# A two-layer trunk on one core: paired visits on TensorE, and the last column in two halves

## The chip, the core and the metric

The kernel runs on one core of a Trainium2 chip. The core has a matrix engine (TensorE, PE), a vector engine (VectorE, DVE), a scalar engine (ScalarE, ACT), GpSimd (POOL) and SyncE (SP). Each has a queue of its own that it works through in order, and each can issue DMAs. TensorE reads its operands from SBUF and writes to PSUM, which has 8 banks of 512 float32 values per partition. The metric is the device time of one execution in microseconds; lower is better.

## What is computed

Two layers and a final norm over 256 tokens of width 2048, in float32:

```python
for i in range(DEPTH):                       # DEPTH = 2
    h = _rms_norm(x, norm_mix[i])
    if i % 2 == 0:
        x = x + _gmlp_mixer(h, ...)          # u * (W_s v + b) in chunks of 128 tokens, then w_out
    else:
        x = x + _s5_mixer(h, ...)            # 128 groups of 16 channels, 64 complex states each
    x = x + _swiglu(_rms_norm(x, norm_ffn[i]), ffn_w1[i], ffn_w3[i], ffn_w2[i])
    gate = jax.nn.sigmoid(_rms_norm(x, norm_ple[i]) @ ple_w_gate[i])
    x = x + gate * (p[i] @ ple_w_proj[i])
return _rms_norm(x, norm_final)
```

In the S5 mixer the states follow a diagonal recurrence, s[t] = a s[t-1] + B u[t], and the output is Re(C s) + d u, then gelu and a gated product.

## The kernel before

**Weight tiles.** All large weights stream through SBUF in 792 tiles of 256 x 512 (`STAGES`, `ORDER`). SyncE loads a tile into RAW, ScalarE writes its rounded copy WHI (line 810), VectorE the rest WLO (line 1096). ScalarE and VectorE are some four tiles ahead of TensorE. TensorE multiplies a tile in 12 matmuls of 512 columns, eight with WHI (line 1616) and four with WLO (line 1622). The operands, in OP, are split in the same way; the helper `high` writes the one part on ScalarE and `low` the other on VectorE. `start(stage, n)` is the number of the first tile of column n of a stage; `split_used` counts the tiles that TensorE has finished.

**Visits.** Small matmuls stand between two tiles, where a table of tile numbers puts them. In the first layer these are the turns of x (`turn`, 0 to 3), two turns of the mixing weights WN (`turn_ws`, at `WT_AT`) and four mixes (`mix`, at `MIX_AT`, all into banks 6 and 7, one per column of stage "us").

**The state stage.** It begins at tile 396, W0, the start of "win" (32 tiles, x into u), and runs into "out1". A step g is the tile W0 + g. Each of the engines has a loop over g in which its jobs stand in a fixed order. The channels go in eight duos d of 256. For a duo:
- TensorE computes the increments of the states from u (`into_states`, lines 1793 on, at `INTO_AT`), and later, from the scanned states, the output (`out_of_states`, lines 1809 on, at `OUT_AT`). Increments of duo d need the tables TQ and the spread input UP; the output needs the tables TD and TK, the states SD, and that ScalarE has taken the output of duo d - 1 from PSUM.
- VectorE takes the increments from PSUM (CV, line 1501) and scans them (lines 1510 to 1525, ten instructions) at `INTO_AT + 1`; at `OUT_AT + 2` it turns the output (YG, line 1532, `turn_y`), and one step later it writes the low part of the operand (line 1537, `y_low`).
- ScalarE takes the output with gelu at `OUT_AT + 1` (YP, line 1011, `take_y`) and writes the high part of the operand at `OUT_AT + 2` (line 1018, `y_high`), for which it waits for YG.
- u comes in four parts of two duos. ScalarE stores part n to DRAM (`ud`, line 995, `store_u`) at step 8n + 11, and at step 8n + 13 it waits for that store and issues four loads that spread it into UP (line 1003, `spread_u`).
- GpSimd loads the tables TQ, TD, TK and TE at the steps of `TQ_AT`, `TD_AT`, `TK_AT` and `TE_AT`, and waits in order for the buffer of each: table TD of duo 5, at step 30, waits for the output of duo 3.

Where a loop has two duos at a step, the lower one's job comes first:

```python
INTO_AT = [W0 + g for g in (16, 19, 24, 27, 32, 34, 40, 42)]
OUT_AT = [W0 + g for g in (20, 23, 28, 31, 36, 38, 44, 46)]
```

**The end.** The last column of "gate1" has all its nine tiles in SBUF. TensorE goes through them once for the first 128 tokens and once for the others, 54 matmuls of 512 columns each (lines 1882 to 1884). Behind each half come a sigmoid (line 1072), product, sum and statistics on VectorE (lines 1589 to 1591), the norm, and the DMA of the output.

## Time and profile before

| | |
|---|---|
| runs | 2236.19, 2233.8, 2236.26 us; median 2236.19 |
| the profiled execution | 2234.53 us, of which the span of the trace is 2232.5 |
| TensorE busy | 2217.6 us, 99% of the span; granted clock 0.999 |
| VectorE busy | 1443.7 us, 65% |
| ScalarE busy | 1024.3 us, 46% |
| GpSimd busy | 493.6 us, 22% |
| DMA | 531.02 MB, mean 238 GB/s |

The span runs from the first to the last instruction of the trace, and the rest of an execution's time lies around it. All rows below come from that one execution, with times in us from the span's start. A row of a timeline is a run of equal instructions: its start, how long it lasts, the engine, the line, the operation, what is written from what, and how often; in brackets how long the engine stood idle before, and what released it. ACTq is a DMA issue from ScalarE's queue. Busy TensorE says little about waits of a fraction of a microsecond, since matmuls overlap in the pipe; the distance between starts tells more.

### The profile page before, as it was taken

The numbers are of one execution on the slowest core, as the hardware profiler recorded it, in microseconds if no ns is written. First come the engines' busy times: TensorE is split into PE (matmuls) and PEld (weight loads), VectorE is DVE, ScalarE is ACT, GpSimd is POOL, SyncE is SP. The second block draws the span as 40 slices with busy tenths as digits, with TensorE's granted clock in tenths as the row PEclk, the third lists the DMA queues.
The fourth block names the chain that finished last, engine by engine and source line by source line (L and its number), as shares of the span: only waits on it lengthen the run. The fifth ranks groups of instructions, "written<-read, shape, count | busy, mean of one in ns | idle before, by whom it ended". The sixth has DMA issues, their size and how long they took to land.

```text
span 2232.5 us, 28320 instructions
## 1 busy us (share of the span) xinstructions
PE 2217.6 (99%) x11226; PEld 1830.5 (82%) x11226; DVE 1443.7 (65%) x1608; ACT 1024.3 (46%) x1233; POOL 493.6 (22%) x470
## 2 busy tenths in 40 slices
PE   9999999999999999999999999999999999999998
PEld 7888888888888888888887788888888888888886
DVE  7878776666666666666668866555555445556665
ACT  5544444444434444445444445544444344444454
POOL 1246145456665534301003100000000000000001
PEclk9999999999999999999999999999999999999999
DMA  8677898988888898888689877777776667777773
GB/s 304 186 207 228 264 283 249 257 249 237 259 248 225 243 280 247 265 244 269 231 261 353 307 227 217 216 223 220 211 218 206 194 194 225 220 210 233 230 233 143
DMA packets 350676, 531.02 MB, mean 238 GB/s; under 512 B 106209, under 2 KB 127089, under 8 KB 349905
## 3 DMA queue, kind: packets, MB, share of 16 engines
q1 hardware_dynamic: 339456, 491.64, 73.7%
q0 software_dynamic: 8320, 30.75, 3.7%
q10 hardware_dynamic: 2768, 6.83, 0.9%
q8 instruction: 88, 1.44, 0.3%
q14 instruction: 44, 0.35, 0.1%
HBM read 475.67 MB, written 53.48 MB: 237 GB/s over the span
## 4 chain that ended last, share of the span: by engine, by line
PE 97%; DMA 1%; DVE 1%; issue 0%; ACT 0%; SPq 0%; ACTq 0%; DVEq 0%
PE PS L1616 63%; PE PS L1622 31%; DMA RAW<-in_s_w_out 1%; DMA HT<-zd 0%; PE PS L1883 0%; PE PS L1884 0%; PE PS L1882 0%; PE PS L1721 0%; PE PS L1647 0%; PE PS L1710 0%; DVE OP L1122 0%; PE PS L1830 0%; PE PS L1805 0%; PE PS L1822 0%; PE PS L1756 0%
## 5 line engine op out<-in xcount | busy, mean ns | idle before, releaser
L1616 PE MATMUL PS<-WHI,OP 128*128 128x512 f32 x6208 | 1538.4, 390 | 0.2
L1096 DVE TENSOR_TENSOR WLO<-RAW,WHI 128x1024 fp32r<-128x1024 f32 x783 | 1016.5, 1312 | 692.7 <-ACT WHI L810 688.1
L1616 PEld LDWEIGHTS PS<-WHI,OP 128*128 128x128 f32 x6208 | 1161.9, 188 | 244.7 <-issue 3.4
L810 ACT ACTIVATE WHI<-RAW 128x1024 fp32r<-128x1024 f32 x783 | 827.9, 1062 | 997.4 <-PE PS L1622 644.4
L1622 PE MATMUL PS<-WLO,OP 128*128 128x512 f32 x3104 | 829.8, 389 | 0.9 <-DVE WLO L1096 0.9
L1622 PEld LDWEIGHTS PS<-WLO,OP 128*128 128x128 f32 x3104 | 582.5, 188 | 122.3 <-DVE WLO L1096 1.4
L794 POOL TENSOR_TENSOR ON<-X,GF 128x1024 f32<-128x1024 f32 x3 | 9.9, 3295 | 941.8 <-DVE X L1448 941.8
L696 POOL TENSOR_TENSOR TA<-BRAW,FAC 128x64 f32<-128x64 f32 x16 | 10.7, 669 | 268.4 <-DMA BRAW<-in_s_b_im 268.3
L858 ACT ACTIVATE S<-PS,RC 128x512 f32<-128x512 f32 x66 | 41.7, 684 | 37.3 <-PE PS L1622 37.1
L1122 DVE SCALAR_TENSOR_TENSOR OP<-HT,VEC,OP 128x128 fp32r<-128x128 f32 x120 | 37.9, 388 | 14.1 <-ACT OP L834 14.0
L1108 DVE TENSOR_TENSOR OP<-HT,OP 128x512 fp32r<-128x512 f32 x50 | 36.2, 764 | 14.5 <-ACT OP L825 14.5
L825 ACT ACTIVATE OP<-HT 128x512 fp32r<-128x512 f32 x50 | 28.8, 624 | 28.3 <-DMA HT<-zd 28.0
L834 ACT ACTIVATE OP<-HT,VEC 128x256 fp32r<-128x256 f32 x60 | 25.6, 498 | 18.9 <-DMA HT<-zd 18.9
L1163 DVE BATCH_NORM_STATS2 STAT<-X 128x6 f32<-128x512 f32 x54 | 34.0, 670 | 0.0
L1435 DVE SCALAR_TENSOR_TENSOR Z<-PS,RC,S 128x512 f32<-128x512 f32 x44 | 30.8, 741 | 4.0 <-PE PS L1622 4.0
L1147 DVE STREAM_TRANSPOSE ZT<-Z 128x512 f32<-128x512 f32 x50 | 32.6, 691 | 0.9
L733 POOL TENSOR_TENSOR TB<-CT,LAMA 128x512 f32<-128x512 f32 x16 | 29.0, 1811 | 0.0
L712 POOL TENSOR_TENSOR QT<-TA,TB 128x512 f32<-128x512 f32 x16 | 27.5, 1717 | 1.3
L1387 DVE TENSOR_TENSOR X<-X,PS 128x1024 f32<-128x1024 f32 x20 | 24.4, 1219 | 4.4 <-PE PS L1622 4.4
L946 ACT ACTIVATE EXPF<-PS 128x128 f32<-128x128 f32 (+7 forms) x128 | 16.8, 319 | 21.1 <-PE PS L1721 21.1
L734 POOL TENSOR_TENSOR DT<-TA,TB 128x512 f32<-128x512 f32 x16 | 25.9, 1618 | 1.3
L732 POOL TENSOR_TENSOR TA<-CT,LAMA 128x512 f32<-128x512 f32 x16 | 25.8, 1612 | 1.3
(214 smaller groups left out, 942.1 us busy)
## 6 DMA issues: line engine op xcount, KB each, us to landing
RAW<-in_ffn_w SPq DMA_DIRECT2D x528, 512.0 KB, 4.4
RAW<-in_gm_w_in SPq DMA_DIRECT2D x64, 512.0 KB, 4.3
RAW<-in_s_w_out SPq DMA_DIRECT2D x64, 512.0 KB, 4.8
RAW<-in_ple_w_gate SPq DMA_DIRECT2D x56, 512.0 KB, 4.7
zd<-ZT SPq DMA_DIRECT2D x40, 512.0 KB, 3.6
HT<-zd SPq DMA_DIRECT2D x160, 128.0 KB, 5.0
RAW<-in_gm_w_out SPq DMA_DIRECT2D x32, 512.0 KB, 5.5
RAW<-in_s_w_in SPq DMA_DIRECT2D x32, 512.0 KB, 4.8
```

The source lines that it names most:

```text
L733: step(G_.tensor_tensor(TB[:, :, :, :], c(0), up(1), ALU.mult))
L810: A_.activation(hi_of(t), raw_of(t), ACT.Copy).then_inc(hi_ready, 1)
L825: A_.activation(OP[:, block_:block_ + QB, P * h:P * h + P].rearrange("p m (i a) -> p m i a", a=32), HT[:, :, :, h, :].rearrange("p i m a - ...
L858: last = A_.activation(dst(th), acc(stage, n)[:, th, :], func, scale=RC[:, RMS[stage], th:th + 1])
L1096: V_.tensor_tensor(lo_of(t), raw_of(t), hi_of(t).bitcast(F32), ALU.subtract).then_inc(lo_ready, 1)
L1108: V_.tensor_tensor(here[:, :, TOK + P * h:TOK + P * h + P].rearrange("p m (i a) -> p m i a", a=32), HT[:, :, :, h, :].rearrange("p i m a - ...
L1122: last = V_.scalar_tensor_tensor(OP[:, b, TOK + P * th:TOK + P * th + P].rearrange("p (i a) -> p i a", a=32), HT[:, :, m, th, :], VEC[:, r ...
L1147: last = V_.transpose(ZT[:, :, :, h, :], src[:, h, :].rearrange("p (m c a) -> p c m a", c=4, a=32))
L1163: last = V_.bn_stats(STAT[:, th, 6 * n:6 * n + 6], src[:, th, NW * n:NW * n + NW])
L1435: last = V_.scalar_tensor_tensor(Z[:, th, :], acc(stage, n)[:, th, :], RC[:, i_rms, th:th + 1], S[:, th, :], ALU.mult, ALU.mult)
L1616: T_.matmul(dst[:, th, :], x_part, hi_of(t)[:, f], start=first and kk == 0 and part == 0, stop=False)
L1622: last = T_.matmul(dst[:, th, :], hi, lo_of(t)[:, f], start=False, stop=last_one and kk == TK - 1)
```

## The change

- **Head.** ScalarE and VectorE write the first half of the first operand, then split weight tile 0, then write the second half. On TensorE the turns 2 and 3 of x both stand behind tile 1 (before: behind tiles 0 and 2).
- **First layer.** Both turns of WN stand behind one tile, into banks 6, 7 and 4, 5. The mixes 0 and 1 share a tile, and 2 and 3, in banks 6 and 4 in turn.
- **State stage.** `INTO_AT` and `OUT_AT` of the first four duos are four tiles apart, so that the increments of duo d + 1 and the output of duo d stand behind one tile for d = 0 to 3, increments first. VectorE's take of the last increments comes one step earlier, right behind the scan of duo 6, and `y_low` of duo 5 one step later. The tables' steps move with them in part.
- **End.** The second 128 tokens of the last column go in two parts of 256 columns each, which have banks of their own; the statistics have a fifth group, and a part of ON is filled ahead.
- GpSimd also waits for six tiles of "up0a" before it clears EXP[1].

```diff
-MIX_AT = [start("us", n) + 6 for n in range(NT)]
+MIX_AT = [start("us", n - n % 2) + 6 for n in range(NT)]
+MIX_BANK = [6, 4, 6, 4]
...
-WT_AT = [start("v", 2) + 2, start("v", 2) + 6]
+WT_AT = start("v", 2) + 2
...
+PARTS = [(0, 0, NW), (1, 0, NW // 2), (1, NW // 2, NW)]
...
-INTO_AT = [W0 + g for g in (16, 19, 24, 27, 32, 34, 40, 42)]
-OUT_AT = [W0 + g for g in (20, 23, 28, 31, 36, 38, 44, 46)]
-
-TAKEN_AT = [t + 1 for t in INTO_AT[:DUOS - 1]] + [INTO_AT[DUOS - 1]]
+INTO_AT = [W0 + g for g in (16, 20, 24, 28, 32, 34, 40, 42)]
+OUT_AT = [W0 + g for g in (20, 24, 28, 32, 36, 38, 44, 46)]
+
+TAKEN_AT = [t + 1 for t in INTO_AT[:DUOS - 1]] + [INTO_AT[DUOS - 1] - 1]
+LOW_AT = [t + 3 + (d == DUOS - 3) for d, t in enumerate(OUT_AT)]
...
-TQ_AT += [(W0 + g, W0 + g + 1) for g in (17, 20, 25, 28, 33, 35)]
+TQ_AT += [(W0 + g, W0 + g + 1) for g in (17, 21, 25, 29, 33, 35)]
...
+                    pool.wait_ge(split_used, start("up0a") + 6)
                     step(G_.memset(EXP[1][:, :, :, :], 0.0))
...
-            high(0)
+            high(0, (0,))
             section()
+            high(0, (1,))
             section()
...
-                    if W0 + g == Y_AT[d] + 1:
+                    if W0 + g == LOW_AT[d]:
                         y_low(d)
...
             def prologue(t):
-                if t in (0, 2):
-                    turn({0: 2, 2: 3}[t])
+                if t == 1:
+                    turn(2)
+                    turn(3)
...
                 for d in range(DUOS):
                     if t == INTO_AT[d]:
                         into_states(d)
+                for d in range(DUOS):
                     if t == OUT_AT[d]:
                         out_of_states(d)
...
-            for th in range(2):
+            for th, c0, c1 in PARTS:
...
-                        f = slice(NW * kk, NW * kk + NW)
+                        f = slice(NW * kk + c0, NW * kk + c1)
```

**TensorE's queue around steps 19 to 24.** First the kernel before. L1805 are increments, L1822 and L1830 an output; SD_126 is the states' buffer of the even duos, SD_127 of the odd ones.

```order
L1805 MATMUL PS<-TQ_114,UP_131 32x64 x32
L1616 MATMUL PS<-WHI,OP 128x512 x8
L1622 MATMUL PS<-WLO,OP 128x512 x4
L1822 MATMUL PS<-TK_118,UP_131 32x128 x16
L1830 MATMUL PS<-TD_115,SD_126 32x128 x32
...
L1822 MATMUL PS<-TK_119,UP_131 32x128 x16
L1830 MATMUL PS<-TD_116,SD_127 32x128 x32
L1616 MATMUL PS<-WHI,OP 128x512 x8
L1622 MATMUL PS<-WLO,OP 128x512 x4
L1805 MATMUL PS<-TQ_113,UP_132 32x64 x32
```

The same place after, where L1825 are increments and L1842 and L1850 an output:

```order
L1636 MATMUL PS<-WHI,OP 128x512 x8
L1642 MATMUL PS<-WLO,OP 128x512 x4
L1825 MATMUL PS<-TQ_114,UP_131 32x64 x32
L1842 MATMUL PS<-TK_118,UP_131 32x128 x16
L1850 MATMUL PS<-TD_115,SD_126 32x128 x32
...
L1642 MATMUL PS<-WLO,OP 128x512 x4
L1825 MATMUL PS<-TQ_113,UP_132 32x64 x32
L1842 MATMUL PS<-TK_119,UP_131 32x128 x16
L1850 MATMUL PS<-TD_116,SD_127 32x128 x32
L1636 MATMUL PS<-WHI,OP 128x512 x8
```

The increments of duo 1 have moved down by a tile, onto the tile behind which the output of duo 0 stands, and the output of duo 1 has moved down by a tile behind the increments of duo 2.

**ScalarE's queue from step 24 on, before.** Z is u being taken from PSUM, YP the output of duo 1, OP<-YG its operand, ud the third store of u, and UP_131<-ud the spread of it:

```order
L858 ACTIVATE Z<-PS,RC 128x512 x2
L1011 ACTIVATE YP<-PS 128x2x16x8 x2
L810 ACTIVATE WHI<-RAW 128x1024
L1018 ACTIVATE OP<-YG 128x2x256
L810 ACTIVATE WHI<-RAW 128x1024 x2
L995 DMA ud<-UT 128x1024
L810 ACTIVATE WHI<-RAW 128x1024 x2
L1003 DMA UP_131<-ud 32x2x512 x4
L1011 ACTIVATE YP<-PS 128x2x16x8 x2
```

The same after:

```order
L869 ACTIVATE Z<-PS,RC 128x512 x2
L821 ACTIVATE WHI<-RAW 128x1024
L1023 ACTIVATE YP<-PS 128x2x16x8 x2
L821 ACTIVATE WHI<-RAW 128x1024
L1030 ACTIVATE OP<-YG 128x2x256
L821 ACTIVATE WHI<-RAW 128x1024
L1007 DMA ud<-UT 128x1024
L821 ACTIVATE WHI<-RAW 128x1024 x2
L1015 DMA UP_131<-ud 32x2x512 x4
L1023 ACTIVATE YP<-PS 128x2x16x8 x2
```

The take of YP, the operand and the tile split between them have moved down by one tile split; the store and the spread of u stand where they stood, now with one split instead of two between the operand and the store.

**VectorE's queue at steps 25 to 27, before.** UT is u turned for the store, YG the turned output of duo 1, CV the increments of duo 2, SD_126 the end of their scan (ten rows from CV to there), OP<-YG the low part of the operand:

```order
L1096 TENSOR_TENSOR WLO<-RAW,WHI 128x1024 x2
L1497 STREAM_TRANSPOSE UT<-Z 128x1024
L1532 STREAM_TRANSPOSE YG<-YP 128x512
L1501 STREAM_TRANSPOSE CV<-PS 128x8x2x32
...
L1525 TENSOR_TENSOR SD_126<-CV,CA 128x8x31
L1096 TENSOR_TENSOR WLO<-RAW,WHI 128x1024
L1537 TENSOR_TENSOR OP<-YG,OP 128x2x256
```

The same after:

```order
L1110 TENSOR_TENSOR WLO<-RAW,WHI 128x1024 x2
L1512 STREAM_TRANSPOSE UT<-Z 128x1024
L1516 STREAM_TRANSPOSE CV<-PS 128x8x2x32
...
L1540 TENSOR_TENSOR SD_126<-CV,CA 128x8x31
L1110 TENSOR_TENSOR WLO<-RAW,WHI 128x1024
L1547 STREAM_TRANSPOSE YG<-YP 128x512
L1110 TENSOR_TENSOR WLO<-RAW,WHI 128x1024
L1552 TENSOR_TENSOR OP<-YG,OP 128x2x256
```

The turn into YG, on which ScalarE's operand waits, stood ahead of the scan of duo 2 and now stands behind it and one more tile split. At steps 33 to 35 the same has happened to the turn of duo 3 and the scan of duo 4.

## Rows read from the trace of the kernel before

**Rows 1.** the page: its span, and the busy time of TensorE
```profile
span 2232.5 us, 28320 instructions
PE 2217.6 (99%) x11226; PEld 1830.5 (82%) x11226; DVE 1443.7 (65%) x1608; ACT 1024.3 (46%) x1233; POOL 493.6 (22%) x470
```

**Rows 2.** timeline, TensorE, state stage: start us, us, engine, line, operation, tiles, count
```profile
1180.02 1.98 PE L1616 MATMUL PS<-WHI,OP 128*128 128x512 f32 x8
1182.74 1.98 PE L1616 MATMUL PS<-WHI,OP 128*128 128x512 f32 x8
...
1185.55 1.08 PE L1822 MATMUL PS<-TK,UP 128*32 128x128 f32 x32
...
1187.65 2.11 PE L1616 MATMUL PS<-WHI,OP 128*128 128x512 f32 x8
```

**Rows 3.** timeline, ScalarE and its DMA issues (ACTq), third store of u
```profile
1192.81 1.18 ACT L1018 ACTIVATE OP<-YG 128x512 fp32r<-128x512 f32 x1 [3.04 <-DVE YG L1532]
...
1194.82 0.33 ACTq L995 DMA_DIRECT2D ud<-UT  x1
...
1203.74 2.62 ACTq L1003 DMA_DIRECT2D UP<-ud  x4
```

**Rows 4.** timeline of VectorE beside it
```profile
1192.10 0.67 DVE L1532 STREAM_TRANSPOSE YG<-YP 128x512 f32<-128x512 f32 x1
1192.70 0.68 DVE L1501 STREAM_TRANSPOSE CV<-PS 128x512 f32<-128x512 f32 x1
...
1194.02 0.69 DVE L1511 TENSOR_TENSOR CB<-CV,TE 128x512 f32<-128x512 f32 x1
1194.74 0.42 DVE L1512 TENSOR_TENSOR CV<-CA,CB 128x256 f32<-128x256 f32 x1
...
1198.94 1.22 DVE L1096 TENSOR_TENSOR WLO<-RAW,WHI 128x1024 fp32r<-128x1024 f32 x1
```

**Rows 5.** line L995 at 1194.5 to 1195.5: that store, issue to landing
```profile
DMA to landing us min/median/max: 8.0/8.0/8.0
```

**Rows 6.** line L1003, 1205.5 to 1206.0: the spread that it feeds
```profile
DMA to landing us min/median/max: 7.6/8.3/8.9
```

**Rows 7.** windows: stretch, busy by engine (count), TensorE clock, DMA share, GB/s
```profile
1200.00:1205.00 5.00, 5.00 (x111) 3.94 (x110) 4.97 (x7) 1.06 (x1) 2.99 (x4) 1.00 1.03 413
```

**Rows 8.** timeline of TensorE: visits of steps 32 and 38, wait of 44
```profile
1219.51 1.10 PE L1805 MATMUL PS<-TQ,UP 128*32 128x64 f32 x64
...
1240.80 1.08 PE L1822 MATMUL PS<-TK,UP 128*32 128x128 f32 x32
...
1262.93 1.08 PE L1822 MATMUL PS<-TK,UP 128*32 128x128 f32 x32 [0.69 <-DVE CV L1501]
```

**Rows 9.** timeline of ScalarE: the fourth store of u and its spread
```profile
1223.88 0.33 ACTq L995 DMA_DIRECT2D ud<-UT  x1
...
1235.02 2.54 ACTq L1003 DMA_DIRECT2D UP<-ud  x4
```

**Rows 10.** timeline of TensorE: the first mix and the tile behind it
```profile
120.44 1.95 PE L1710 MATMUL PS<-V,WT 128*128 128x128 f32 x16
122.14 2.08 PE L1616 MATMUL PS<-WHI,OP 128*128 128x512 f32 x8
```

**Rows 11.** timeline of all engines: the end of the program
```profile
2223.04 0.69 ACT L1072 ACTIVATE S<-PS,RC 128x512 f32<-128x512 f32 x1 [5.46 <-PE PS L1884]
...
2223.76 0.69 DVE L1589 TENSOR_TENSOR Z<-S,PS 128x512 f32<-128x512 f32 x1 [8.31 <-ACT S L1072]
...
2227.01 1.15 ACT L1079 ACTIVATE ON<-ON,RC 128x1024 f32<-128x1024 f32 x1 [0.23 <-DVE RC L1596]
```

**Rows 12.** windows of TensorE: the 54 matmuls of the last row half
```profile
2210.62:2223.00 12.38, 12.38 (x55) 1.00 0.20 85
```

**Rows 13.** timeline of all engines: the start
```profile
9.15 2.08 PE L1616 MATMUL PS<-WHI,OP 128*128 128x512 f32 x8
...
15.59 0.76 POOL L643 DMA_DIRECT2D PN<-in_p  x1 [5.16 <-DMA X<-in_x]
```

More of the change, by code:

```diff
@@ L270, in trunk @@
         RHO = place("RHO", [P, PAIRS])
-        STAT = place("STAT", [P, 2, 4 * 6])
+        STAT = place("STAT", [P, 2, 5 * 6])
         MV = place("MV", [P, 2, 2])
@@ L469, in acc, with gate_of, proj_of @@
             return PS[:, b:b + 2, :]
+        def gate_of(th, c0, c1):
+            bank = BANKS["gate1", NT - 1] + th if c0 == 0 else 4
+            return PS[:, bank, c0:c1]
+        def proj_of(th, c0, c1):
+            return PS[:, 6 + th if c0 == 0 else 5, c0:c1]
         def feature_major(bank, h):
@@ L819, in high @@
                     act.wait_ge(ht_in, 64 * (MOVED.index(q) + 1))
-                for h in range(2):
+                for h in halves:
                     if bank is not None:
@@ L1067, in _ @@
             until(TILES)
-            for th in range(2):
-                act.wait_ge(half_done, th + 1)
-                A_.activation(S[:, th, :], acc("gate1", NT - 1)[:, th, :], ACT.Sigmoid, scale=RC[:, 5, th:th + 1]).then_inc(half_s, 1)
+            for i, (th, c0, c1) in enumerate(PARTS):
+                act.wait_ge(half_done, i + 1)
+                A_.activation(S[:, th, c0:c1], gate_of(th, c0, c1), ACT.Sigmoid, scale=RC[:, 5, th:th + 1]).then_inc(half_s, 1)
+                if c1 < NW:
+                    continue
                 act.wait_ge(ms_ready, 7 + th)
@@ L1100, in until, with low @@
                     section()
-            def low(q):
+            def low(q, halves=(0, 1)):
                 stage, n, _, block_, row, _, bank = QUADS[q]
-                for h in range(2):
+                for h in halves:
                     dve.wait_ge(operand_hi, 2 * q + h + 1)
@@ L1166, in moments @@
             def moments():
-                V_.bn_aggr(MV[:, 0, :], STAT[:, 0, :])
-                step(V_.bn_aggr(MV[:, 1, :], STAT[:, 1, :]))
+                V_.bn_aggr(MV[:, 0, :], STAT[:, 0, 0:6 * NT])
+                step(V_.bn_aggr(MV[:, 1, :], STAT[:, 1, 0:6 * NT]))
                 step(V_.tensor_tensor(MSQ[:, :], MV[:, :, 0], MV[:, :, 0], ALU.mult))
@@ L1585, in _ @@
             until(TILES)
-            f = slice(3 * NW, D)
-            for th in range(2):
-                dve.wait_ge(half_s, th + 1)
-                step(V_.tensor_tensor(Z[:, th, :], S[:, th, :], PS[:, 6 + th, :], ALU.mult))
-                step(V_.tensor_tensor(X[:, th, f], X[:, th, f], Z[:, th, :], ALU.add))
-                step(V_.bn_stats(STAT[:, th, 6 * NT - 6:6 * NT], X[:, th, f]))
-                step(V_.bn_aggr(MV[:, th, :], STAT[:, th, :]))
+            for i, (th, c0, c1) in enumerate(PARTS):
+                f = slice(3 * NW + c0, 3 * NW + c1)
+                chunk = 6 * (NT - 1 + (c0 > 0))
+                dve.wait_ge(half_s, i + 1)
+                step(V_.tensor_tensor(Z[:, th, c0:c1], S[:, th, c0:c1], proj_of(th, c0, c1), ALU.mult))
+                step(V_.tensor_tensor(X[:, th, f], X[:, th, f], Z[:, th, c0:c1], ALU.add))
+                if c1 < NW:
+                    V_.tensor_tensor(ON[:, th, f], X[:, th, f], GF[:, f], ALU.mult)
+                step(V_.bn_stats(STAT[:, th, chunk:chunk + 6], X[:, th, f]))
+                if c1 < NW:
+                    continue
+                step(V_.bn_aggr(MV[:, th, :], STAT[:, th, 0:chunk + 6]))
                 V_.scalar_tensor_tensor(MS[:, th:th + 1], MV[:, th, 0:1], MV[:, th, 0:1], MV[:, th, 1:2],
@@ L1709, in mix @@
                         h = QB * n + m
-                        last = T_.matmul(PS[:, 6 + th, P * m:P * m + P], WT[:, h, :], V[:, th, P * h:P * h + P], start=True, stop=True)
+                        last = T_.matmul(PS[:, MIX_BANK[n] + th, P * m:P * m + P], WT[:, h, :], V[:, th, P * h:P * h + P], start=True, stop=True)
                 last.then_inc(mixed, 1)
@@ L1771, in first_layer @@
                     turn_p(0)
-                for i in range(2):
-                    if t == WT_AT[i]:
-                        turn_ws(i)
+                if t == WT_AT:
+                    turn_ws(0)
+                    turn_ws(1)
                 for n in range(NT):
@@ L1867, in _ @@
             free("gate1", NT - 1)
-            for th in range(2):
+            for th, c0, c1 in PARTS:
                 for j in range(DEEP):
```

30 lines of the change are left out of this document (15 added, 15 removed).

## The prediction

> **What bounds the kernel now.** The page comes first: TensorE is busy 2217.6 of 2232.5 us [rows 1], so the program is TensorE's queue of matmuls, and a change can only shorten the two ends, the gaps around the small matmuls, or the waits. The timeline of TensorE comes second. A weight tile (12 matmuls of 512 columns) repeats every 2.72 us, as 1180.02 to 1182.74 shows [rows 2]. Only the places between tiles can move. Third come the timelines of ScalarE and VectorE around the state stage, because each works through its own queue in order there and feeds the visits. I count steps in that stage as the code does: step g is the weight tile W0 + g.
>
> **Merged visits of the state stage.** Step 23's tile should have ended at 1182.74 + 2.72 = 1185.46; the output visit starts at 1185.55, and the tile behind it takes 2.11 us instead of 1.98 for its first part [rows 2]. So a visit costs 0.09 + 0.13 = 0.22 us beyond its own matmuls. Four increments now share a tile with the output of the duo before: 4 x 0.22 = 0.9 us less (up to 1.5, if the drain of the small matmuls shrinks too). The last duo's increments are now taken before two other VectorE jobs, so the wait of 0.69 us at step 44 [rows 8] goes, 0.7 us. What is late next there is the scan of the same duo, which has two steps more.
>
> **Merged visits of the first layer.** The first mix issues 16 matmuls in 1.95 us and the next tile starts 1.70 us after the first of them [rows 10]. With 16 at about 0.11 us that is their own work, so merging two of four mixes, the two turns of WS and two turns of X gives at most 0.1 us. I take 0.1.
>
> **The head.** Tile 0 starts at 9.15 [rows 13]. Its weight split no longer stands behind the second half of the first operand, which I take as 0.3 us (bounds 0 and 0.4). From 8.85 two tiles run to 14.3 and the turn of the third quarter of X, now ahead of tile 2, to about 15.2. The last quarter of X is there just before 15.59, where GpSimd, which waited for it, goes on [rows 13]. That wait gives the 0.3 us back. Sum 0, bounds -0.3 and +0.3. The new wait of GpSimd for tile 101 costs nothing: it is over before C has come back from DRAM.
>
> **The tail.** Behind the last matmul stand a sigmoid, three VectorE operations of 512 columns, and small ones [rows 11]. At 256 columns a VectorE operation takes 0.42 instead of 0.69 us [rows 4]: 3 x 0.27 = 0.8 us. The sigmoid (0.69) loses about 0.2. The scaling of ON on ScalarE (1.15 us) stays and hides VectorE's wider one. Against it stands TensorE: 54 matmuls of 512 columns take 12.38 us, 0.229 each [rows 12]; now 108 of 256. If the cost is all columns they are free. If the part beyond half of 0.229, as 0.013 us of fixed cost, is paid twice, they cost 54 x 0.013 = 0.7 us. No row has such a matmul with this operand type; the far bound is 0.188 us each, a weight load's length, +7.9 us. The small f32 matmuls with a full weight load run at 0.11 us apart [rows 10], so I take +0.4. Tail: -0.6 (bounds -1.0 and +0.1 without the far one).
>
> The Trainium skill, "TensorE: Matmul & The Clock Gate", section "Back-to-back issue gap", gives a gap of columns / 2.4 + 2.5 ns: 109 ns for 256, which by an estimate from that page would make the 108 matmuls 0.6 us shorter than they are now. The trace's 0.229 us for 512 is over the page's 0.216, so the measured row is what I use.
>
> **What moves behind what.** This is the term that decides. Before, VectorE turned the output of duo 1 (YG, 1192.10) before it took the increments of duo 2 (CV, 1192.70) and worked through them until 1198.94 [rows 4]. ScalarE writes the operand as soon as YG is there (1192.81), splits a tile and stores u for the third time at 1194.82 [rows 3]. After, OUT 1 stands at step 24 and its turn at step 26, behind the scan of step 25. ScalarE stands in its queue at the operand of duo 1 meanwhile, and the store of u, two entries further on, stands behind it.
>
> Worked through, in times of the trace before: the scan still starts at about 1192.6. It gets a split more in front of it, but the increments are there earlier. So YG starts at 1192.6 + 6.2 + 1.15 = 1200.0, the operand follows 0.7 later, and the store at 1201.8 (one tile split fewer than the 2.72 us of [rows 3, 4]). The store takes 8.0 us to land [rows 5], at 1209.8. The spread takes 2.6 us to issue [rows 3], and its last part 8.3 more to land [rows 6]: about 1220. The increments of duo 4 at step 32 need it. TensorE comes there at 1179.8 + 3 x 2.72 = 1188.0, then two merged visits of 3.4 us and eight tiles of 2.72, at 1216.6. It waits there for some 3.5 us. Before, the same data were there at 1214.6, for a visit at 1219.51 [rows 8].
>
> The same happens once more for the fourth u. ScalarE is free of the third spread at 1212.4. The output of duo 2 and a split (2.1), a split and YG on VectorE (1.2), its operand and three ScalarE jobs beside five of VectorE put the scan of duo 4 at 1224.1. It ends at 1230.4, YG of duo 3 starts at 1231.5, and the store is at 1233.3 (it was 1223.88 [rows 9]). With 8.0 us to land and 2.6 for the spread, ScalarE takes the output of duo 4 from PSUM at 1243.9 to 1245.1, and OUT 5 at step 38 needs that bank. OUT 5 was at 1240.80 [rows 8]; it is now 4.3 us later, whatever the stall at step 32 was, because this chain doesn't run through TensorE. Tile 40 needs the output of duo 5, for 0.6 us more. With the 0.7 us of step 44 the stage ends 4.3 + 0.6 - 0.7 = 4.2 us later; the merged visits are within this, since they only let TensorE come earlier to the wait.
>
> **The sum** against the profiled execution (2234.53 us, span 2232.5): +4.2 - 0.1 + 0 - 0.6 = +3.5, so 2238.0 us. The median of the runs shown is 1.7 above that execution, at 2236.19; the same +3.5 gives 2239.7. About 0.2%, 4.5 us, is what a measurement of this kernel can tell from no change, so the forecast is a small loss inside it.
>
> **Rivals.**
> 1. The store and spread land in time. The chain has two landings of 8 us, taken while the DMA engines are full (share 1.03 [rows 7]). If GpSimd, which now waits for OUT 3 before its table loads, leaves the engines free and each landing took 4 us, both stalls vanish and what is left is -0.9 - 0.7 - 0.1 - 0.6 = -2.3: 2233.9. For it: the engines' load does fall in that gap. Against it: the tile loads alone keep them busy, and two stores in a row would have to be fast. Beside it, the Trainium skill, "DMA: Bandwidth & Descriptors", section "Anatomy of one DMA — SWDGE (gpsimd) path", fits 2.0 us plus bytes / 436e3 (for GpSimd's path). For 512 KB that is an estimate of 3.2 us a landing and this rival's time. The trace shows 8.0.
> 2. Slower by more than can be missed: GpSimd's table loads behind OUT 3 (one step later, and later still by the stall) and the fourth spread meet in one burst. The spread then lands 2 to 4 us after ScalarE issued it later than I take, and the increments of duo 6 at step 40 wait as well. They are due only about 1 us after the spread's landing. From 1 us more on each landing it decides. 4.2 + 3 - 0.7 = +6.5: 2242.7.
> 3. The short matmuls go by the weight load (0.188 us): +7.9 in place of +0.4 in the tail, 2247. The 0.11 us spacing of full weight loads [rows 10] speaks against it.
> 4. The merging does nothing for a visit (the 0.22 us stay) and the tail gains nothing: within 1 us of the forecast, since the chain above sets the stage anyway. It is part of the forecast's case.
>
> **How the numbers follow.** Forecast 0.63, rival 1 0.18, rival 2 0.15, rival 3 0.04. The forecast's case alone runs from 2237.5 to 2242, by 1 us each way on the two landings and the tail's bounds. A fifth of it lies over 2240.7. Slower: 0.15 + 0.04 + 0.13 = 0.32. Faster needs a time below 2231.7, under rival 1's own value: 0.03. Same: 0.65. The range takes in rival 1's value and nearly all of rival 2's: 2233.0 to 2242.7.
>
> **What would show it.** In the timeline after: the third store of u about 7 us later relative to the tile of step 27 than before; TensorE idle before the increments of step 32 by 2 to 5 us and before the output of step 38 by 1 to 4; no wait at step 44; ScalarE's longest waits for YG; and behind the last matmul 1 us less than the 9 us now. It would be wrong if the store of u went out before the scan of duo 2 ended, if its landing took under 5 us, or if the 108 matmuls took over 13 us.

## The result: 2238.8 us against 2236.0

The changed kernel takes 2238.81 us (median of 22 runs, 2237.33 to 2242.11), the kernel before 2236.03 us (22 runs). The ratio is 1.0014, with a 95% interval of 1.0008 to 1.002: a small loss, 2.8 us between the medians and 0.14% by the ratio (its interval is 1.8 to 4.5 us), under the prediction's bound of 0.2%. All profile readings below are of one execution each. The one of after takes 2239.38 us, its span is 2237.3 us against 2232.5.

The page of after, its span, the busy engines, and the queue of instruction fetches (queue, kind, packets, MB, share), which answer to [rows 1]:

```profile
span 2237.3 us, 28436 instructions
PE 2218.9 (99%) x11280; PEld 1835.7 (82%) x11280; DVE 1450.4 (65%) x1612; ACT 1023.4 (46%) x1234; POOL 492.9 (22%) x470
...
q8 instruction: 89, 1.46, 0.3%
```

TensorE's timeline of after at step 20 (start us, us, engine, line, operation, tiles, count; in brackets the idle time before and its releaser). Increments, output and the next tile, where before had one visit with 0.22 us around it [rows 2]:

```profile
1175.22 1.10 PE L1825 MATMUL PS<-TQ,UP 128*32 128x64 f32 x64
...
1177.13 1.06 PE L1850 MATMUL PS<-TD,SD 64*32 64x128 f32 x52
1179.16 0.44 PE L1850 MATMUL PS<-TD,SD 64*32 64x128 f32 x12 [0.96 <-issue]
1179.53 2.11 PE L1636 MATMUL PS<-WHI,OP 128*128 128x512 f32 x8
```

The output stops for 0.96 us after 52 of its last 64 matmuls, and no other engine is named. The same timeline at steps 32, 38 and 40 (before: [rows 8]):

```profile
1219.08 1.10 PE L1825 MATMUL PS<-TQ,UP 128*32 128x64 f32 x64 [0.20 <-issue]
...
1220.99 1.16 PE L1850 MATMUL PS<-TD,SD 64*32 64x128 f32 x64
1224.53 2.09 PE L1636 MATMUL PS<-WHI,OP 128*128 128x512 f32 x8 [2.38 <-ACT WHI L821]
...
1246.15 1.08 PE L1842 MATMUL PS<-TK,UP 128*32 128x128 f32 x32 [1.45 <-ACT YP L1023]
...
1251.92 2.11 PE L1636 MATMUL PS<-WHI,OP 128*128 128x512 f32 x8 [0.65 <-ACT YP L1023]
```

Behind the visit of step 32 TensorE stands still for 2.4 us, at the output of step 38 for 1.45, ahead of tile 40 for 0.65. The releaser "WHI" of the first is not to be believed: ScalarE had finished that tile's split at 1214.69, 9.8 us earlier.

ScalarE's timeline of after, with its DMA issues, at the third and the fourth store of u (before: [rows 3], [rows 9]):

```profile
1201.75 1.17 ACT L1030 ACTIVATE OP<-YG 128x512 fp32r<-128x512 f32 x1 [6.01 <-DVE YG L1547]
1201.90 0.33 ACTq L1007 DMA_DIRECT2D ud<-UT  x1
...
1209.80 2.79 ACTq L1015 DMA_DIRECT2D UP<-ud  x4
...
1232.75 1.16 ACT L1030 ACTIVATE OP<-YG 128x512 fp32r<-128x512 f32 x1 [8.62 <-DVE YG L1547]
1232.89 0.33 ACTq L1007 DMA_DIRECT2D ud<-UT  x1
...
1242.28 2.55 ACTq L1015 DMA_DIRECT2D UP<-ud  x4
1244.93 1.08 ACT L1023 ACTIVATE YP<-PS 128x256 f32<-128x256 f32 x2 [4.72 <-issue]
```

VectorE's beside it: the take of the increments of duo 2, and YG, which now stands behind their scan (before: [rows 4]):

```profile
1193.63 0.67 DVE L1516 STREAM_TRANSPOSE CV<-PS 128x512 f32<-128x512 f32 x1
...
1201.01 0.70 DVE L1547 STREAM_TRANSPOSE YG<-YP 128x512 f32<-128x512 f32 x1
```

Line L1007 at 1201.5 to 1202.5, the third store, issue to landing (before: [rows 5]):

```profile
DMA to landing us min/median/max: 7.9/7.9/7.9
```

The first merged mix, which answers to [rows 10]:

```profile
121.47 3.73 PE L1729 MATMUL PS<-V,WT 128*128 128x128 f32 x32
124.96 1.40 PE L1636 MATMUL PS<-WHI,OP 128*128 128x512 f32 x5
```

The end. First TensorE's windows (stretch, us, busy (count), clock, DMA share, GB/s), the last column's first and second half, then ScalarE and VectorE behind the last matmul. They answer to [rows 12] and [rows 11]:

```profile
2203.55:2215.88 12.33, 12.33 (x56) 1.00 0.00 0
2215.88:2228.83 12.95, 12.95 (x109) 1.00 0.20 82
```

```profile
2228.86 0.47 ACT L1084 ACTIVATE S<-PS,RC 128x256 f32<-128x256 f32 x1 [5.45 <-PE PS L1905]
...
2229.44 0.42 DVE L1605 TENSOR_TENSOR Z<-S,PS 128x256 f32<-128x256 f32 x1 [4.32 <-ACT S L1084]
...
2231.92 1.15 ACT L1093 ACTIVATE ON<-ON,RC 128x1024 f32<-128x1024 f32 x1 [0.23 <-DVE RC L1616]
```

**Where the time went.** Positions of TensorE's tiles, after against before: tile 0 at +0.47 us, tile 18 at +1.06, tile 76 (behind the mixes) at +0.95, the tile of step 16 at +1.40, the tile behind the last output at +5.33, the same until the last column, and the end at +4.86. So the state stage, from the tile of step 16 (412) to tile 446, is 3.92 us longer, and the end 0.47 shorter. The +1.0 of the head is told of under the experiments.

### The profile page after: what moved, and what is told of

Read it like the earlier page. It is cut to its first block, busy times and chain, and to the rows that moved or that the text cites. A ratio compares the mean times of both kernels' runs of the same rounds, so it can differ in the third digit from the quotient of the medians.

```text
span 2237.3 us, 28436 instructions
## 1 busy us (share of the span) xinstructions
PE 2218.9 (99%) x11280; PEld 1835.7 (82%) x11280; DVE 1450.4 (65%) x1612; ACT 1023.4 (46%) x1234; POOL 492.9 (22%) x470
## 4 chain that ended last, share of the span: by engine, by line
PE 94%; DMA 2%; DVE 2%; issue 1%; ACT 0%; ACTq 0%; SPq 0%; DVEq 0%
PE PS L1636 61%; PE PS L1642 31%; DMA ud<-UT 1%; DMA HT<-zd 0%; PE PS L1667 0%; PE PS L1904 0%; DVE WLO L1110 0%; PE PS L1905 0%; PE PS L1903 0%; DMA RAW<-in_s_w_in 0%; PE PS L1740 0%; PE PS L1729 0%; DVE OP L1136 0%; DMA X<-in_x 0%; ACT WHI L821 0%
## 5 line engine op out<-in xcount | busy, mean ns | idle before, releaser
L770 POOL DMA_DIRECT2D TD<-tabd x16 | 8.6, 539 | 86.7 <-PE PS L1642 69.8
```

## The experiments

The profiled executions side by side, in us. "Head" is the start of tile 18; "step 38" is the start of the output there, counted from the start of the tile of step 16; "stage" is tile 412 to tile 446; "median" is of all runs. Each ratio is against runs of the kernel before that were made beside the kernel of its row. Their medians go from 2235.42 to 2236.25 us, so the medians of two rows may differ by some 0.8 us for that reason alone, and the ratios say more.

| kernel | head | step 38 | stage | median | ratio (95% interval) |
|---|---|---|---|---|---|
| before | 61.51 | 81.92 | 122.21 | 2236.03 | |
| after | 62.58 | 85.87 | 126.13 | 2238.81 | 1.0014 (1.0008 to 1.002) |
| e_states | 61.54 | 84.56 | 125.37 | 2237.87 | 1.0015 (1.0006 to 1.0023) |
| e_rest | 61.36 | 82.36 | 125.73 | 2236.4 | 1.0002 (0.9993 to 1.0011) |
| e_store | 61.04 | 83.11 | 124.75 | 2238.33 | 1.001 (1.0001 to 1.0019) |
| e_shift | 61.28 | 85.94 | 127.80 | 2239.07 | 1.0017 (1.0008 to 1.0026) |
| e_turn | 61.71 | 82.60 | 123.99 | 2236.36 | 1.0005 (0.9996 to 1.0014) |
| e_turn_take | 61.47 | 82.39 | 123.34 | 2236.6 | 1.0003 (0.9994 to 1.0012) |
| e_fit | 61.24 | 83.19 | 126.39 | 2237.25 | 1.0005 (0.9996 to 1.0014) |
| e_fit_take | 61.30 | 82.20 | 123.78 | 2235.74 | 1.0 (0.9991 to 1.0009) |
| e_two | 62.70 | 81.05 | 121.83 | 2234.89 | 0.9996 (0.9987 to 1.0005) |
| e_pads | 61.41 | 92.31 | 135.51 | 2247.05 | 1.0047 (1.0033 to 1.0061) |
| e_both | 61.70 | 92.17 | 131.47 | 2244.5 | 1.0036 (1.0023 to 1.005) |
| e_turn_pads | 61.26 | 90.97 | 131.67 | 2243.44 | 1.0034 (1.0022 to 1.0046) |

**e_states and e_rest: which part loses.** The first is the kernel before with the state stage of after:

```diff
-INTO_AT = [W0 + g for g in (16, 19, 24, 27, 32, 34, 40, 42)]
-OUT_AT = [W0 + g for g in (20, 23, 28, 31, 36, 38, 44, 46)]
+INTO_AT = [W0 + g for g in (16, 20, 24, 28, 32, 34, 40, 42)]
+OUT_AT = [W0 + g for g in (20, 24, 28, 32, 36, 38, 44, 46)]
...
                     if t == INTO_AT[d]:
                         into_states(d)
+                for d in range(DUOS):
```

> The kernel before with the state stage of after alone (tables of steps, increments ahead of the output, the late low part). Theory A (the state stage loses, by the store of u that waits in ScalarE's queue for YG): the stretch from the increments of step 16 to the tile behind the last output grows by 3.9 us as in the trace of after, everything else stands where it stood before, ratio 1.0017, about 2240. Rival B (the loss is spread over the program, the head and the mixes carry 1.0 to 1.4 of it): the same 3.9 in the stage, but then the other parts must lose too, see e_rest. Theory F on the two gaps in it (TensorE runs out of fetched instructions in the dense merged visits): the gaps of 0.96 us in the visit of step 20 and of 2.4 us behind that of step 32 are here too, at the same place in TensorE's instruction stream (the stream is 1 instruction shorter up to there). If the gap of step 32 comes from a wait for data it may move by tenths or vanish.

The second is the reverse, after with these tables and this loop as before:

> After with the state stage of before: head, merged mixes and turns, and the tail alone. Theory A: the head and the mixes cost nothing, the +1.0 us by the first mix in the trace of after is the later rise of TensorE's granted clock in that one execution (11.1 us against 6.1), so only the tail's -0.5 and the mixes' -0.1 are left: -0.6, ratio 0.9997, about 2235.4. Rival B (the head costs what the trace of after showed, +0.9 to +1.3): +0.4 to +0.7, 2236.5 or more, and the tile behind the first mix is 1 us later than before also with the clock up at 6 us.

The state stage alone costs what the whole change costs: 1.0015 against 1.0014, a stage 3.2 us longer, and the two stops of TensorE at the same matmuls (1.08 us in the visit of step 20, 0.57 behind that of step 32). The rest alone can't be told from no change, 1.0002; the gain of 0.6 us that was expected of it lies inside its interval, but is not seen.

The head is settled by many profiles. The head of after stands in eleven more kernels of this study; in ten of them tile 18 starts between 61.04 and 61.71 (mean 61.38), and with the old head at 61.51 and 61.54. Only in after (62.58) and in e_two (62.70) it is a microsecond later, and there TensorE is still slow in tile 0. TensorE's timeline of after, to be held against the 2.08 us of [rows 13]:

```profile
8.00 1.97 PE L1667 MATMUL PS<-IDENT,X 128*128 128x128 f32 x8 [0.61 <-DMA X<-in_x]
9.62 2.79 PE L1636 MATMUL PS<-WHI,OP 128*128 128x512 f32 x8
```

The eight matmuls take 2.79 us and the turn of eight tiles of x 1.97, which other executions do in 2.08 and 1.09. The first record of the full granted clock in this trace is at 11.1 us, in that of before at 6.1, in that of e_two, which has the same slow tile 0, at 11.4. The program's start ahead of that is the same instructions, so the time at which the clock rises is the execution's, and the +1.06 of the head in after's trace is not the change's.

What e_rest's profile adds was not expected: its stage is as long as after's, though its order is that of before. Windows of TensorE in e_rest, around step 44:

```profile
1262.00:1265.50 3.50, 1.28 (x6) 1.00 1.04 373
1265.50:1268.00 2.50, 2.41 (x64) 0.58 0.95 352
```

The output of step 44 had to wait for 2.31 us instead of the 0.69 of [rows 8], and behind that wait the granted clock is 0.58 of full in the stretch of 2.5 us. Single executions of the same order differ by 3 us in this way. It may be why the runs of one kernel spread over 4 to 5 us, and it is why I read mechanisms, not sums, from the profiles.

**e_store: the store of u ahead of the waiting operand.**

```diff
-                    if W0 + g == U_AT[n] + 2:
+                    if W0 + g == U_AT[n] + 1:
                         store_u(n)
```

> After with each store of u one step earlier in ScalarE's queue, so that it stands ahead of the operand of the output that waits for YG. Theory A: third store near 1194 instead of 1201.9, fourth near 1223 instead of 1232.9, the waits of 1.45 us at the output of step 38 and 0.65 behind tile 39 go, as does the 0.25 us at the increments of step 32; the gaps of 0.96 and 2.4 us stay. -2.2 us against after, 2236.6. Rival C (the 2.4 us behind step 32 are a wait for data of the same late chain): that gap goes too, -4.5 us or more, 2234.3.

The stores go out at 1192.18 and 1222.48, and the output of step 38 starts 2.8 us earlier than in after, with 0.18 us of wait. Theory A holds to that point. But the time is hardly less (ratio 1.001 against 1.0014, with intervals that overlap), and a wait of 2.06 us stands ahead of tile 40. ScalarE's timeline of e_store, the operand of duo 4 and the take of the output of duo 5, and TensorE's tile 40:

```profile
1245.62 1.14 ACT L1030 ACTIVATE OP<-YG 128x512 fp32r<-128x512 f32 x1 [5.07 <-DVE YG L1547]
...
1247.61 1.04 ACT L1023 ACTIVATE YP<-PS 128x256 f32<-128x256 f32 x2
```

```profile
1248.70 2.11 PE L1636 MATMUL PS<-WHI,OP 128*128 128x512 f32 x8 [2.06 <-ACT YP L1023]
```

ScalarE stood 5.07 us at the operand of duo 4, for YG, and the take of duo 5 is queued behind it. YG in turn waits in VectorE's queue: without the turn ahead of the scan of duo 4, VectorE ends that scan, splits, turns, and then idles 2.17 us for a split that ScalarE has queued behind its own operand, so that it takes the increments of duo 5 at 1234.98, before at 1232.04. The late store was one consequence of the order, not all of it. Rival C, that the stop behind step 32 is a wait for data, is not decided here: that stop shrank to 0.56 us but did not go, and that of step 20 stayed at 1.06. The next experiment decides it.

**e_shift: 112 instructions that do nothing.**

```diff
+IDLE = {g: 28 for g in range(4, 12)}
...
+            def idle(t):
+                for _ in range(IDLE.get(t - W0, 0)):
+                    pe.wait_ge(exp_ready, KB)
...
+                idle(t)
                 tile(t, acc(stage, n), OPERAND[stage][0] + TK * j, j == 0, j == 7)
```

(Two such waits become one instruction.)

> After with 112 more instructions in TensorE's queue (waits that are long fulfilled) spread over steps 4 to 11; no data, job or order changes. Theory F (instructions are fetched in blocks of 256, boundaries at the place 194 of each; a merged visit of 321 instructions whose first boundary comes within its first 70 instructions or so runs through the next block before it is there): the gaps in the visit of step 20 and behind that of step 32 vanish (their first boundaries now at instruction 185 and 209 of the visit), and a new gap of 1 to 2.5 us appears in the visit of step 24, at its instruction 278. Time within 1.5 us of after, about -1. Rival C (a wait for data): both gaps stay where they are, none appears at step 24, time as after, or up to 2 us more if the added waits cost TensorE something.

How the places are counted: each recorded matmul is two instructions in TensorE's queue, its weight load and itself, and each wait that stands alone is one. The trace of after then has 22822 instructions, and its page shows 89 fetches of 16 KB, one for each 256 of them; before has 22713 and 88 fetches, e_pads 23211 and 90. In after the matmul behind the stop at step 20 is instruction 11458 and the one behind the stop at step 32 is 12738 or 12739: five times 256 apart. In e_states, e_store, e_turn and e_turn_take the stops stand before the same two matmuls, and the one stop of e_rest before the second of them. TensorE's timeline of e_shift at step 24:

```profile
1189.30 0.89 PE L1851 MATMUL PS<-TD,SD 64*32 64x128 f32 x42
1190.79 0.63 PE L1851 MATMUL PS<-TD,SD 64*32 64x128 f32 x22 [0.60 <-issue]
```

Both stops are gone, and a new one of 0.60 us is where it was foretold, at the next boundary, though shorter than the 1 us or more that was expected. So the stops are instruction fetches, not data; no data moved in this edit. A merged visit runs through 256 instructions in some 2.4 us. In the state stages of all profiles, each block that was run through in under 3 us, the stop left out, has such a stop (0.6 to 2.4 us) behind it. With separate visits a block takes some 5 us or more, and the loss at the boundary behind step 32 is 0.15 us in before and 0.6 in e_rest. One longer block had a stop of this kind too, 0.8 us in e_pads; its fetch began 5.8 us after TensorE had entered the block ahead.

The second lesson is in the table. The output of step 38 starts 85.94 us after step 16, in after 85.87, though TensorE has no stops of 0.96 and 2.4 us on the way. It waits for 3.42 us there instead of 1.45. The rest of the difference went into the stop of 0.60 us and into a wait at step 34, which after doesn't have, for a table of the increments. TensorE's timeline of e_shift there:

```profile
1226.34 1.10 PE L1826 MATMUL PS<-TQ,UP 128*32 128x64 f32 x64 [1.02 <-DMA TQ<-tabq]
```

So in after the stops cost nothing up to step 38: the chain through VectorE, ScalarE and the DMAs sets that time. It is also why the time is after's and not the 1 us less that I had thought.

**e_turn: the turn back ahead of the scan.**

```diff
+TURN_AT = [t + (1 if d in (1, 3) else 2) for d, t in enumerate(OUT_AT)]
...
-                    if W0 + g == OUT_AT[d] + 2:
+                    if W0 + g == TURN_AT[d]:
                         turn_y(d)
```

> After with the turn of the output (YG) of duos 1 and 3 one step earlier in VectorE's queue, ahead of the scans of duos 2 and 4, as the kernel before had it. Theory A2 (what e_store showed: without the turn ahead of the scan not only the store of u but also ScalarE's operand and, through the low part and the split behind it, VectorE's take of the increments of duo 5 come 3 us late, and the take of the output of duo 5 with them): third store about 1198, fourth about 1226, no wait over 0.5 us at the output of step 38 nor behind tile 39; against that the scans of duos 2 and 4 start 1 to 3 us later than in e_store, up to 1 us of wait at the outputs of steps 28 and 36. Gaps at block boundaries as in after, 0.7 to 2.4 us together. State stage +1 to +2 over before, 2236.5. Rival (the turn is not what makes it late; the merged visit alone does, since output and increments now end together): the waits at step 38 and tile 40 stay within 1 us of after's 2.1 us, 2238.5.

This one edit of two places takes about 2 of the 2.8 us back: 2236.36 us, ratio 1.0005 against 1.0014. The intervals of these two overlap, but all nine kernels without padding behind a visit that have merged visits agree. The five with the turn of duo 1 ahead of the scan (e_turn, e_turn_take, e_fit, e_fit_take, e_two) are at 0.9996 to 1.0005, the four without it (after, e_states, e_store, e_shift) at 1.001 to 1.0017. The output of step 38 starts 82.60 us after step 16, 3.3 us earlier than in after, and the stage is 2.1 us shorter. ScalarE's timeline of e_turn, the operand and store of duo 1, and later the split of a weight tile beside which the fourth spread is issued:

```profile
1194.66 1.17 ACT L1031 ACTIVATE OP<-YG 128x512 fp32r<-128x512 f32 x1
...
1195.84 0.33 ACTq L1008 DMA_DIRECT2D ud<-UT  x1
...
1238.11 1.06 ACT L822 ACTIVATE WHI<-RAW 128x1024 fp32r<-128x1024 f32 x1 [9.68 <-DMA RAW<-in_s_w_out]
```

The operand doesn't wait for YG any more, and the store stands 36.3 us behind the tile of step 16, in after 41.6. What was missed: a wait of 1.78 us ahead of tile 40 is still there, in this execution since a weight tile came late (9.68 us of ScalarE's idle time), and the take of the output stands behind its split.

**e_turn_take: and that take one step earlier.**

```diff
-TURN_AT = [t + (1 if d in (1, 3) else 2) for d, t in enumerate(OUT_AT)]
+TURN_AT = [t + (1 if d in (1, 3, 4) else 2) for d, t in enumerate(OUT_AT)]
...
-                    if W0 + g == OUT_AT[d] + 1:
+                    if W0 + g == OUT_AT[d] + (d != 5):
                         take_y(d)
```

> The same earlier turn and take on top of e_turn, without the added instructions. The gaps at block boundaries stay (about 1 us each at steps 20 and 32), the wait behind tile 39 is under 1 us: 1 us less than e_turn, 2235.5; against e_fit_take it is the price of the two gaps, 0.5 to 2 us more.

No wait ahead of tile 40, as foretold, and e_fit (2.06 us there) and e_fit_take (none) differ in the same way. But the outputs of steps 44 and 46 now wait for 0.71 and 0.77 us, for VectorE, where e_turn has no wait, so most of it is lost again. In the time there is nothing to see (2236.6).

**e_pads, e_both, e_turn_pads: padding that costs more than it saves.** All three put 93 instructions between each two merged visits, 23 ahead of each tile, so also directly behind the visit; e_both adds the earlier store, e_turn_pads the turn of e_turn.

```diff
-IDLE = {g: 28 for g in range(4, 12)}
+IDLE = {**{g: 27 for g in range(4, 12)}, **{g: 46 + g % 2 for g in range(21, 33)}}
```

> After with 389 more instructions in TensorE's queue (waits long fulfilled): 107 over steps 4 to 11, and 93 between each two of the merged visits, so that in all four of them the first block boundary (place 194 of 256) comes at instruction 188 to 190 of the visit and the next behind it, in the tile. Theory F (blocks of 256 instructions fetched too late): no gap over 0.3 us at any such boundary, at steps 20, 24, 28 and 32. The queue chain of ScalarE stays, so the wait at the output of step 38 takes over what the gap behind step 32 gave: state stage 1 to 2 us shorter than in after, 2237.5. Rival (the gaps have another cause): gaps of 1 to 2.4 us at two of the four visits as before, and the time no shorter than after's 2238.8; the added waits may cost up to 2 us.

> The store of u one step earlier and the added instructions of e_pads. Theory F: no gap at a block boundary. Theory A2: the wait behind tile 39 for the output of duo 5 stays, as in e_store (2.1 us there), and grows by what TensorE gains before it, up to 3 us, since it hangs on VectorE's and ScalarE's queues: 2237.5 to 2238.3. Rival (the wait behind tile 39 in e_store came from the fetch gap of step 32): it shrinks to under 1 us, 2236.

> Both edits: the turn of duos 1 and 3 ahead of the scans, and the added instructions of e_pads. If both theories hold, the state stage loses neither to the queue nor to the fetches, and the 4 x 0.36 us of the merged visits and the tail's 0.5 us show: 1.5 to 3 us less than before, 2233.5, ratio 0.999. If the merged visits have another cost that neither edit touches, it stays at or above the kernel before, 2236.

Measured: 2247.05, 2244.5 and 2243.44 us, ratios 1.0047 (1.0033 to 1.0061), 1.0036 (1.0023 to 1.005) and 1.0034 (1.0022 to 1.0046). Eleven of the twelve boundaries in question are free of a stop, but each merged visit is followed by another. TensorE's timeline of e_pads behind step 20:

```profile
1176.02 1.16 PE L1851 MATMUL PS<-TD,SD 64*32 64x128 f32 x64
1179.39 1.86 PE L1637 MATMUL PS<-WHI,OP 128*128 128x512 f32 x7 [2.21 <-issue]
```

2.2 us for 23 instructions that do nothing, 0.1 us each. I take it that TensorE's sequencer has no lead behind a dense visit, so that every instruction shows; no run separates this from another cause. Three visits make 6.6 us. So my expectation of at most 2 us was wrong by this, and the rival that the added waits cost time was right. What the three say of each other is little: the state of the queues is another in them.

**e_fit and e_fit_take: padding only inside tiles.** 23 instructions ahead of each of the three tiles before steps 24, 28 and 32, none behind a visit, and 15 ahead of each of twelve tiles; the second with the edit of e_turn_take.

```diff
-IDLE = {**{g: 27 for g in range(4, 12)}, **{g: 46 + g % 2 for g in range(21, 33)}}
+IDLE = {**{g: 30 for g in range(4, 16)}, **{4 * b + r: 46 for b in (5, 6, 7) for r in (2, 3, 4)}}
```

> e_turn with 387 added instructions in TensorE's queue (waits long fulfilled), 15 in each of the tiles 4 to 15 and 23 in each of the three tiles before steps 24, 28 and 32, none directly behind a merged visit, where e_pads showed each to cost 0.1 us. The first block boundary of the merged visits comes at instruction 117, 141, 166 and 190. Theory F: no gap at a block boundary (e_turn has 1.0 and 0.9 us at steps 20 and 32), nothing added elsewhere; the waits of ScalarE's and the weights' side stay. 0.5 to 2 us less than e_turn, 2235. Rival (the added instructions cost time inside tiles too): the tiles with 23 of them take more than 2.72 us, and the time is 2238 or more.

> e_fit, and beside it the turn of the output of duo 4 and ScalarE's take of the output of duo 5 one step earlier. If the wait of 2.2 us behind tile 39 in e_turn comes from the splits ahead of that take in ScalarE's queue, it falls to under 1 us: 1 us less than e_fit, 2234. If it comes from the weights that are late for those splits, the wait moves to the next tile and nothing is won.

All four merged visits of both kernels are clean: visit and tile together take 5.80 to 5.83 us at steps 20, 24, 28 and 32, where after has 7.11, 5.80, 5.80 and 8.52. But some of the padded tiles now stop. TensorE's timeline of e_fit:

```profile
1200.65 2.09 PE L1638 MATMUL PS<-WHI,OP 128*128 128x512 f32 x8 [1.04 <-issue]
```

The place of that matmul is 18 instructions behind a boundary, all of them padding. But the fetch of that block had ended 3.4 us before TensorE went on, so this stop is not shown to be a late fetch; its cause is open. The fitted kernels are at 2237.25 (1.0005, 0.9996 to 1.0014) and 2235.74, where 2235 and 2234 were expected. So the fetches can be kept out of the visits, and filling the queue is no way to win by it.

**e_two: what the runs point to.** The visits of steps 24 and 28 merged, those of duos 0 and 3 apart as before; turn of duo 1, turn of duo 4 and take of duo 5 early; 32 instructions ahead for the phase.

```diff
-INTO_AT = [W0 + g for g in (16, 20, 24, 28, 32, 34, 40, 42)]
-OUT_AT = [W0 + g for g in (20, 24, 28, 32, 36, 38, 44, 46)]
+INTO_AT = [W0 + g for g in (16, 19, 24, 28, 32, 34, 40, 42)]
+OUT_AT = [W0 + g for g in (20, 24, 28, 31, 36, 38, 44, 46)]
...
+TURN_AT = [t + (1 if d in (1, 4) else 2) for d, t in enumerate(OUT_AT)]
+IDLE = {g: 8 for g in range(4, 12)}
```

> What the runs point to: after's head, mixes and tail; in the state stage only the visits of steps 24 and 28 merged (duos 0 and 3 as before, at 19/20 and 31/32), the turn of duo 1 ahead of the scan of duo 2, the turn of duo 4 and the take of duo 5 one step earlier, and 32 added instructions over steps 4 to 11, so that the first block boundary comes at instruction 102 and 196 of the two merged visits. If the theories of the queue and of the fetch are complete, the state stage has no gap at a block boundary and ends 0.7 us (2 x 0.36) earlier relative to its start than in the kernel before, within 1 us, and with 0.2 from the head and mixes and 0.5 from the tail the time is 1.4 less: 2234.4, ratio 0.9994. If the merged visits make the queues late by themselves, waits of 1 us or more at steps 38, 40 or 44 take that back: 2236 or more.

2234.89 us (2233.31 to 2239.2; before beside it 2236.25), ratio 0.9996, interval 0.9987 to 1.0005: the lowest ratio of the study, but not shown to be faster than before. TensorE's timeline at step 24, without a stop:

```profile
1192.25 1.10 PE L1827 MATMUL PS<-TQ,UP 128*32 128x64 f32 x64
1193.16 1.06 PE L1844 MATMUL PS<-TK,UP 128*32 128x128 f32 x32
1194.15 1.16 PE L1852 MATMUL PS<-TD,SD 64*32 64x128 f32 x64
1195.24 2.11 PE L1638 MATMUL PS<-WHI,OP 128*128 128x512 f32 x8
```

Against before, the steps 23 and 24 take 8.52 us instead of 8.88 and so do 27 and 28: 0.36 us a merged visit. At steps 32, 39, 40 and 44 it is 0.15, 0.09, 0.14 and 0.11 less. Against it stands a wait at step 46 (0.83 more). Sum -0.38, and the stage is 121.83 us against 122.21.

## Why the prediction was right

**The sum.** Forecast were +3.5 us and 2239.7; measured are +2.8 us by the medians and 2238.8. In order of the terms, with the times of after's trace lessened by the 1.40 us that TensorE is later at step 16, to stand in the frame of the forecast:

- **The chain of the state stage, +4.3 at step 38: the path right, +3.95, the size in part by luck.** OUT 5 was forecast at 1245.1 and is at 1244.75. On the way two parts were off and cancel. The scans began earlier, so the fourth store went out at 1231.5 and not at 1233.3; and it took 9.4 us to land, not 8.0. In e_states, whose state stage is the same, that store landed in 7.9 us, about what the forecast took, and the output of step 38 is only 2.64 us later than in before. The third store was 1.3 us early as well (1200.5, forecast 1201.8), with 7.9 us to land. e_turn shows that the turn behind the scan is the cause, since undoing it alone moves OUT 5 back by 3.3 us and takes back about 2 us of the time. e_store shows that the store is not the only way in which it acts: the operand and VectorE's next take are late as well. The prediction named ScalarE's queue, and did not see that second way.
- **The stall at step 32: place right, cause wrong, as costless as foretold.** I had 3.5 us of waiting for UP. UP was there 2.4 us earlier than forecast (the store 1.3 early, its spread's last part 7.0 us to land instead of 8.3; the 8.3 is the median of two parts in [rows 6], and the later one took 8.9), and TensorE waited 0.2 us. What stood there was the fetch of instructions, 2.4 us, which no row of before shows. That it cost nothing is what the prediction said of any stall there, "because this chain doesn't run through TensorE", and e_shift bears it out: without it the output of step 38 is no earlier.
- **Tile 40, +0.6: +0.7. Step 44, -0.7: -0.76**, no wait is left there. Stage: 3.92, forecast 4.2.
- **The merged visits, 0.22 each: 0.36.** A merged one takes 3.08 us and 0.13 of restart against 1.12 + 2.19 + 0.26. The drain of the small matmuls did shrink. Two of the four lost it at once to a fetch, and the others to the wait of step 38. e_two keeps it, for two visits.
- **First layer, -0.1: -0.12** in all twelve kernels with the merged mixes (tile 18 to tile 76, 167.65 us against 167.77). **Head, 0: -0.13 in the mean** of the ten at full clock.
- **Tail, -0.6: -0.47**, the same in every profile within 0.02. The 108 matmuls start 0.118 us apart and cost 0.60, forecast 0.4; behind the last one it is 1.07 us less, forecast 1.0. No row shows the fixed cost of 0.013 us of the prediction's other bound; the runs show 0.011 for each pair, by the 0.60 us above. The bound for a spacing by the weight load (+7.9) is out.

The formula of the Trainium skill ("TensorE: Matmul & The Clock Gate", section "Back-to-back issue gap"), 109 ns for 256 columns, which the page gives for an isolated matmul, is 9 ns under what these pairs of weight load and matmul show.

**The rivals.** The first, landings of 4 us, did not come about: 7.9 and 9.4 us. The Trainium skill, "DMA: Bandwidth & Descriptors", section "Anatomy of one DMA — SWDGE (gpsimd) path", has the fit that the prediction used, by which 3.2 us is an estimate for a transfer of that size on GpSimd's path. The same store took 3.7 us in before as the first of its four (DMA share 0.89), 2.9 us as the fourth in e_both (share 0.68), and 10.6 us as the fourth in e_turn (share 0.98): here the size says little. The second, the increments of duo 6 waiting too, did not come about. The fourth was wrong in its first half, for a visit does gain, and right in that nobody would see it.

**What stays open.** The medians put after 0.9 us below the forecast's sum, which is inside their interval. Behind tile 107, where a weight tile comes late in every profile but that of e_states (waits of 0.7 to 2.1 us), the 0.3 us of head and mixes are not seen any more; the two profiles with the old first layer have 22.98 and 21.76 us there (tile 100 to 108), the twelve with the new one, after among them, 22.75 to 25.02. Whether the new order or chance makes that difference, no run separates. It may be why e_rest is not below before.

## What to carry to other kernels

Before two jobs are put behind one tile, look at the jobs of the other engines that hung on their distance: here VectorE's order "turn, then scan" became "scan, then turn", and through ScalarE's in-order queue, in which DMA issues stand behind waiting work, stores that were 6 and 8 us late reached TensorE as 4 us. Count instructions where small matmuls are packed: here TensorE ran out of fetched code where a whole block of 256 fell on a visit of 321. And before costing a stall at its length, find what sets the time of the next meeting point; stops of 3.3 us in all were free here.

## What the hardware showed beyond that

**A wait can cost twice.** At or behind some waits of TensorE (2.03 us in e_states, 2.06 in e_fit, 2.13 in e_two, 2.31 in e_rest, 3.42 in e_shift) the granted clock went down to the lower of its two levels, 1.2 GHz, for some microseconds. Windows of TensorE, first of e_shift around the output of step 38, then of e_fit around tile 40, then of e_two around tile 107:

```profile
1240.00:1244.00 4.00, 0.87 (x4) 0.90 1.04 392
1244.00:1248.00 4.00, 3.71 (x96) 0.50 1.03 394
1248.00:1252.00 4.00, 4.00 (x21) 0.75 1.05 385
```

```profile
1249.00:1251.00 2.00, 0.30 (x2) 1.00 1.03 388
1251.40:1253.00 1.60, 1.60 (x7) 0.93 1.03 398
1253.00:1255.00 2.00, 2.00 (x6) 0.50 1.04 397
```

```profile
316.00:319.00 3.00, 0.87 (x4) 0.93 1.11 328
319.00:322.00 3.00, 3.00 (x8) 0.50 0.67 233
322.00:325.00 3.00, 3.00 (x15) 1.00 0.52 169
```

The extra time of the 512-column matmuls alone was 0.6, 1.0 and 1.2 us. The waits of 2.38 us in after and 2.06 in e_store were not followed by it, so it is not sure to come. The Trainium skill, "TensorE: Matmul & The Clock Gate", section "HAM oscillation — how this bites in real kernels", says that waiting for data can send TensorE back to its lower clock; these windows agree. The prediction left it out, and in after's profiled execution nothing of it is to be seen in the state stage.

**Fetches of instructions.** By the packets of that queue in the traces one takes 0.9 to 1.9 us, and 0.9 to 1.6 us pass from its end until a stopped TensorE goes on. In the merged visits it began 0.5 to 1.5 us after TensorE had entered the block ahead, but at step 32 of after 2.7 us (DMA share 0.86 from 1220 to 1222 us, 0.39 from there to the end of the stop). Why it came so late there is open.
